# Value products of the decode stage: from a split fp32r form over all output partitions to plain fp32 in four strips of 32

## The reference, cut to what matters

```python
def sample_attn(q, k, v, lam, k_past, v_past, rel_bias):
    ...
    s_past = diff_logits(q, q_pos, k_past, jnp.arange(past, dtype=jnp.int32), rel_bias)
    s_new = diff_logits(q, q_pos, k, q_pos, rel_bias)
    w = diff_weights(jnp.concatenate([s_past, s_new], axis=-1), lam).astype(v.dtype)
    return (jnp.einsum('bhqk,bkhe->bqhe', w[..., :past], v_past)
            + jnp.einsum('bhqk,bkhe->bqhe', w[..., past:], v))
```

## Time and profile before

| what | value |
|---|---|
| timed runs | 2044.92, 2045.65, 2045.75 us; median 2045.65 |
| span of the profiled execution, first to last instruction | 2043.6 us |
| median less that span | 2.05 us |
| instructions | 36009 |
| mean granted TensorE clock | 0.997 |
| sampled stage, from the first key transposes to the last value product | about 835 to 1077 us of the span |

### The profile page before, as it was taken

The page is one execution under the profiler, slowest core; times in us unless marked ns, Lnnn a source line. Parts: engine busy times, 40 slices in busy tenths (PEclk is TensorE's granted clock), DMA queues, the critical chain, the costliest instruction groups (busy, mean ns, idle before and its releaser), DMA issues. The chain is left out here.

```text
span 2043.6 us, 36009 instructions
## 1 busy us (share of the span) xinstructions
PE 1993.2 (98%) x11888; PEld 1850.2 (91%) x11888; DVE 1375.8 (67%) x2932; ACT 998.2 (49%) x1770; POOL 131.7 (6%) x158
## 2 busy tenths in 40 slices
PE   6999999999999999799999999999999999999998
PEld 6999999999999999688878799999999998989896
DVE  6766776767676767678785376675757474847476
ACT  5756575757565757677874242222313141313133
POOL 0000000000000000145560000000000000000000
PEclk9999999999999999999999999999999999999999
DMA  6411111112121112788873131111112020202012
GB/s 199 144 57 54 57 53 56 53 60 59 50 59 50 59 52 87 261 306 304 316 268 92 38 93 42 53 42 42 52 32 62 22 72 22 72 21 69 6 53 99
DMA packets 167453, 183.26 MB, mean 90 GB/s; under 512 B 11045, under 2 KB 139589, under 8 KB 167349
## 3 DMA queue, kind: packets, MB, share of 16 engines
q1 hardware_dynamic: 166137, 181.24, 27.1%
q10 hardware_dynamic: 1212, 0.81, 0.1%
HBM read 162.82 MB, written 24.46 MB: 92 GB/s over the span
## 5 line engine op out<-in xcount | busy, mean ns | idle before, releaser
L1250 PE MATMUL ps<-h_hi,w_hi 128*128 128x384 f32 (+1 forms) x1152 | 386.7, 336 | 5.0 <-DVEq L967 3.4
L1250 PE MATMUL ps<-h_hi,w_lo 128*128 128x384 f32 (+1 forms) x1152 | 376.5, 327 | 0.0
L1250 PE MATMUL ps<-h_lo,w_hi 128*128 128x384 f32 (+1 forms) x1152 | 376.4, 327 | 0.0
L2456 PE MATMUL ps<-h_hi,f_w_hi 128*128 128x320 f32 (+1 forms) x1136 | 370.7, 326 | 0.8 <-PEq L1579 0.8
L2456 PE MATMUL ps<-h_hi,f_w_lo 128*128 128x320 f32 (+1 forms) x1136 | 370.4, 326 | 0.0
L2456 PE MATMUL ps<-h_lo,f_w_hi 128*128 128x320 f32 (+1 forms) x1136 | 370.2, 326 | 0.0
L2535 ACT ACTIVATE yc<-ps,f_prm 128x384 f32<-128x384 f32 x144 | 93.5, 653 | 560.6 <-PE ps L2456 400.0
L2436 PE MATMUL ps<-d_hi,act 128*128 128x512 f32 x816 | 257.0, 390 | 0.5 <-issue 0.5
L1250 PEld LDWEIGHTS ps<-h_hi,w_hi 128*128 128x128 f32 x1152 | 217.0, 188 | 9.0 <-issue 4.0
L1250 PEld LDWEIGHTS ps<-h_lo,w_hi 128*128 128x128 f32 x1152 | 217.1, 188 | 0.6
L1250 PEld LDWEIGHTS ps<-h_hi,w_lo 128*128 128x128 f32 x1152 | 216.8, 188 | 0.0
(11 more groups left out here) (310 smaller groups left out, 3525.2 us busy)
## 6 DMA issues: line engine op xcount, KB each, us to landing
k<-in_cache_k SPq DMA_DIRECT2D x64, 512.0 KB, 5.9
v_raw<-in_cache_v SPq DMA_DIRECT2D x64, 512.0 KB, 4.7
w_raw<-in_w_in SPq DMA_DIRECT2D x48, 512.0 KB, 4.0
f_raw<-in_w_up SPq DMA_DIRECT2D x48, 512.0 KB, 4.0
f_raw<-in_w_down SPq DMA_DIRECT2D x24, 512.0 KB, 3.5
bias<-bias_tiles_dram SPq DMA_DIRECT2D x8, 576.0 KB, 3.6
merged_dram<-mg SPq DMA_DIRECT2D x8, 544.0 KB, 2.7
ow_raw<-in_w_out SPq DMA_DIRECT2D x8, 512.0 KB, 7.5
```

The lines of the kernel that those rows point to most:

```text
L1250: last_ = pe.matmul(bank(s)[:, 0:n], w[:, W_SLOT[g], k, :], x[:, k, off:off + n], start=(k == 0 and i == 0), stop=(k == KT - 1 and i == 2))
L2456: l_ = pe.matmul(ps[:, e % 6, 0:n], w[:, p, k, :], x[:, k, off:off + n], start=(k == 0 and i == 0), stop=(k == KT - 1 and i == 2))
```

## The change

Values stay as they were loaded, in plain fp32. `v_hi`, `v_lo`, `vn` and the split of the weights are gone, with their ScalarE, VectorE and GpSimd instructions. `pt_sb` holds 64 weight columns a page. Each page has two matmuls, one for each half of the value columns: heads 0 to 3 need only rows 0 to 31 of the weights and value columns 0 to 511, heads 4 to 7 rows 32 to 63 and columns 512 to 1023, so the stationary operand is 32 columns and the output 32 partitions. Half `hf` of an even or an odd page goes into strip `2 * hf + n % 2` of one bank; four strips of 32 partitions. `o2` is one bank of 512 columns, `copy_o2` copies 512 columns, `fold_heads` makes 4 transposes, and `fold_rows` adds an even and an odd strip in two instructions.

```diff
-SPLIT_AT = {2: (0, 1), 3: (2,), 4: (3,), 5: (4, 5), 6: (6,), 7: (7,)}
-PV_EARLY = {5: (2,)}
-PV_AT = {4: (0, 1), 5: (), 6: (3,), 7: (4,), 8: (5, 6, NPAGES)}
+PV_EARLY = {}
+PV_AT = {4: (0, 1, 2, 3), 5: (), 6: (), 7: (), 8: (4, 5, 6, NPAGES)}
...
-    pt_both = sb("pt_both", [128, NPAGES + 1, 2, NS], F32R, 158784)
-    o2s = sb("o2s", [128, D], F32, 163392)
+    pt_sb = sb("pt_sb", [128, NPAGES + 1, NS], F32, 158784)
+    o2s = sb("o2s", [128, 512], F32, 163392)
...
+    def strip(hf, n):
+
+        q = 2 * hf + n % 2
+        return o2[32 * q:32 * q + 32, :]
...
-                for g in range(H):
+                for g in range(HH):
                     last = pe.transpose(o2[:, 128 * g:128 * (g + 1)], o2s[:, 128 * g:128 * (g + 1)], c.ident[:, :])
...
                 if n == NPAGES:
-                    pe.wait_ge(new_lo, 2)
-                elif n in POOL_PAGES:
-                    pe.wait_ge(vplo_done, pool_low(b, ("v", n)))
+                    pe.wait_ge(vn_in, 32)
                 else:
-                    pe.wait_ge(vlo_done, len(DVE_PAGES) * (b - 1) + DVE_PAGES.index(n) + 1)
+                    pe.wait_ge(v_in[n], 16 * b)
                 for hf in range(2):
                     cols = slice(512 * hf, 512 * (hf + 1))
-                    parts = (v_hi[:, n, cols], v_lo[:, n, cols]) if n < NPAGES else (vn[:, cols],)
-                    for x, v in enumerate(parts):
-                        last = pe.matmul(o2[:, cols], pt_both[:, n, :, :].rearrange("p a n -> p (a n)"), v,
-                                         start=(n == 0 and x == 0), stop=(n == NPAGES - 1 and x == 1))
+                    v = v_raw[:, n, cols] if n < NPAGES else vn_raw[:, cols]
+                    last = pe.matmul(strip(hf, n), pt_sb[:, n, 32 * hf:32 * hf + 32], v,
+                                     start=(n < 2), stop=(n in (NPAGES - 1, NPAGES)))
...
-                    if has(b, 1):
-                        for n in splits_of(b).get(h, ()):
-                            act.wait_ge(v_in[n], 16 * b)
-                            act.activation(v_hi[:, n, :], v_raw[:, n, :], ACT.Copy).then_inc(vhi_done, 1)
...
-                        for n in splits_of(b).get(h, ()):
-                            if n in POOL_PAGES:
-                                continue
-                            dve.wait_ge(vhi_done, 8 * (b - 1) + n + 1)
-                            dve.tensor_tensor(v_lo[:, n, :], v_raw[:, n, :], v_hi[:, n, :].bitcast(F32),
-                                              ALU.subtract).then_inc(vlo_done, 1)
```

More of the change, by code:

```diff
@@ L1406 @@
 OUT_LOW = [x for x in OUT_SPLITS if x[0] == "m" or x[1] >= 4]
-POOL_LAST = [x for h in range(H + 1)
-             for x in [("v", n) for n in SPLIT_AT.get(h, ()) if n in POOL_PAGES]
-             + [x for x in OUT_AT.get(h, ()) if x not in OUT_LOW]]
+POOL_LOW = [x for h in range(H + 1) for x in OUT_AT.get(h, ()) if x not in OUT_LOW]
 def sampled_and_out(nc, sb, sem, ins, outs, c):
@@ L1418, in sampled_and_out @@
     pt = ps[:, 5, :]
[L1419 to L1423, removed]
+    o2 = ps[:, 6, :]
+    ptn = ps[:, 7, 0:NS]
     v_raw = sb("v_raw", [128, NPAGES, D], F32, 32768)
@@ L1547, in bank_of, with pool_low @@
         return 3 if t == 0 else 0 if t % 2 else 2
[L1549 to L1559, removed]
+    def pool_low(what):
+        return POOL_LOW.index(what) + 1
     def all_turns(eng, body):
@@ L1809, in body @@
                         if h == 4:
-                            pe.wait_ge(ptlo_done, 2 * b)
+                            pe.wait_ge(pthi_done, 2 * b)
                         for n in PV_AT[h]:
@@ L1941, in body @@
                             queries(b + 1, 0)
-                    if h == HH + 1 and isinstance(b, int) and b == 1:
-                        act.wait_ge(vn_in, 32)
-                        act.activation(vn[:, :], vn_raw[:, :], ACT.Copy).then_inc(new_hi, 1)
                     if h == 1 and has(b, 2):
@@ L2056, in fold_rows @@
                 dve.wait_ge(ot_done, b + 1)
-                dve.reduce_sum(oT[:, :, bass.ds(DEC_T * b, DEC_T)], own_rows, mybir.AxisListType.X)                   .then_inc(ots_done, 1)
+                for hf in range(2):
+                    last = dve.reduce_sum(oT[:, HH * hf:HH * (hf + 1), bass.ds(DEC_T * b, DEC_T)], own_rows(hf),
+                                          mybir.AxisListType.X)
+                last.then_inc(ots_done, 1)
             def split_out(what, i):
@@ L2082, in body @@
                         keys(b, h)
-                    if h == 3 and has(b, 1):
-                        dve.wait_ge(pthi_done, 2 * b)
-                        dve.tensor_tensor(pt_lo[:, 0:NPAGES, :], pt.rearrange("p (n k) -> p n k", n=NPAGES),
-                                          pt_hi[:, 0:NPAGES, :].bitcast(F32), ALU.subtract).then_inc(ptlo_done, 1)
-                        dve.tensor_tensor(pt_lo[:, NPAGES, :], ptn, pt_hi[:, NPAGES, :].bitcast(F32),
-                                          ALU.subtract).then_inc(ptlo_done, 1)
                     if at_start(b) and h == 0:
@@ L2096, in body @@
                         queries(b, HH)
-                    if h == HH + 1 and isinstance(b, int) and b == 1:
-                        dve.wait_ge(new_hi, 2)
-                        dve.tensor_tensor(vn[NS:128, :], vn_raw[NS:128, :], vn[NS:128, :].bitcast(F32),
-                                          ALU.subtract).then_inc(new_lo, 1)
                     if h == HH and has(b, 0):
```

35 lines of the change are left out of this document (10 added, 25 removed).

## The result

Four runs of the changed kernel took 2016.15 to 2017.32 us, median 2016.62; four runs of the kernel before beside them had a median of 2045.29 us. The ratio of the times after to before is 0.9858, 95% interval 0.9844 to 0.9872: 28.7 us or 1.4% faster. The forecast was 2046.4 us. The time lies inside its range (2008 to 2076), and close to the 2012.5 us of the first rival.

A forecast was written before the change was run, and what follows sets the result against it. TensorE, busy 98% of the span, was taken as the bound. Seven bodies +4.2, last values 0.0 and body 7 -3.5 gave +0.7 us on the 2043.6 span; with 2.05 to the median, 2046.4 us, range 2008 to 2076.

The forecast's parts named there:

- the first rival: Value products: passes of four strips overlap fully, 4.3 us a sequence in place of 8.6; 2012.5 us, chance 0.29.
- The pairs of half-height matmuls: Earlier trace at 713.42: two matmuls on different array halves take 0.23 us together, as much as one full one.
- value products: Steady sequence: 18 fp32 matmuls on TensorE, only neighbouring passes overlapping, 8.6 us against 7.95, so +0.65 us.
- changes of shape, two runs: TensorE switching array shape, 0.09 us there and 0.14 back, for two value runs a body: +0.45 us.
- `fold_heads`: Transposes on TensorE fall from 8 to 4: -0.4 us a sequence.
- stalls: TensorE waits a sequence: +0.75 us at three heads newly without cover, -0.85 removed; sum taken as -0.1.
- The last values: Body 8: all 18 value matmuls as one run, with shape change and smaller fold, change the time by 0.0 us.
- Body 7: Its 2.41 us wait for `kt_lo` and half clock go, -4.1; output projection splits on uncovered heads, +0.6; together -3.5 us.
- the third rival: Passes overlap in pairs, but loads of narrow stationary operands no longer hide: +29 us on the forecast, 2075; chance 0.08.
- the second: Rival for the value products: strips served one after another, nothing overlaps, 15.5 us a sequence; 2102.7 us, chance 0.17.
- The readout of scores: Between scores: it needs 2.04 us, which a run of values with a head's transposes (3.9 + 0.8 or 1.7 + 0.8) covers.
- faster: Outcome for the whole kernel: a time lower by over 0.2%, given chance 0.38.

The follow-up runs named there:

- strip_by_strip: Changed kernel with the value matmuls of a run sorted by strip, so that passes of one strip stand behind one another; 2025.44 us, ratio 0.9897.
- pairs: Changed kernel with shorter runs of value matmuls: pages 0-1, 2-3 and 4-5 at h = 4, 5, 6, the rest at 8; 2022.83 us, ratio 0.9895.
- before_no_splits: Kernel before, with value splits made for the first sequence only (high parts alone) and reused later; TensorE's instructions unchanged; 2037.44 us, ratio 0.9959.
- gpsimd_only: Changed kernel with only the four GpSimd value subtractions a sequence kept, on a constant tile, read by nobody; 2027.42 us, ratio 0.9908.
- subtractions_kept: Changed kernel with four VectorE and four GpSimd value subtractions a sequence still made, read by nobody, no ScalarE copies; 2042.66 us, ratio 0.9984.
- two_in_a_row: Changed kernel with matmuls sorted by strip, but the new positions as their own run, so no strip has three in a row; 2018.42 us, ratio 0.9867.

## Why the prediction was wrong

**The step that failed.** "I take 8.6, because in all rows here matmuls start in the order of the program and a second fp32 pass starts when the first has streamed." The second half holds, the first doesn't carry over. The rows have no case where a pass waits for its strip while another strip is free. There TensorE doesn't hold back: the term is 4.3 us, its lower bound, and it was priced at twice that. The pairs of half-height matmuls had one pass each and couldn't tell. The Trainium skill, "TensorEngine Tiling (Array Packing)", Key Properties, says that tiles work independently; the trace agrees, four strips in one pass's 0.43 us. The Trainium skill, "TensorE: Matmul & The Clock Gate", Part 3, The mechanism, has matmuls start strictly in program order; here the measurement decides against it, since in strip_by_strip all four strips start at 947.8 (eight loads at 947.82), ahead of three waiting passes of the first.

**Term by term**, for a steady sequence:

| term | predicted | measured |
|---|---|---|
| value products | +0.65 | 4.3 - 7.95 = -3.65 |
| changes of shape, two runs | +0.45 | 0.09 in (942.21 to 943.33, against 1.03), 0.12 to 0.13 out: +0.43 |
| `fold_heads` | -0.4 | -0.4 |
| stalls | -0.1 (-1.5 to +0.8) | 24.7 - 21.7 - 2.2 = +0.8 |
| sum | +0.6 | -2.8 |

The 21.7 are 14.56 for the heads, 4.3, 0.43, 2.03 and 0.4. Pass price, the sum of the two changes of shape, and fold were right. (The 0.14 us back could not be read from the earlier trace rows: they give only four passes and the change together, 1.86 us.) The stalls came out at the top of their bounds. I counted three new heads without cover at 0.24 us, and 0.85 us of old stalls that go. There are four such heads in a row, 2.07, 2.15, 2.15 and 2.18 us from start to start, together 1.2 us over issue and shape; so only about 0.4 us of the old stalls went. The waits around the fold (0.42 and 0.44) stayed, as said.

**The rest.** The last values: predicted 0.0, measured 4.42 - 7.93 - 0.4 = -3.9, the same failed step. Body 7: the 2.41 us wait and the half clock went, as said. It gained 5.0 us, 2.2 more than a steady one, where 3.5 more were forecast (4.1 less 0.6). Loads from memory came in time: 338 GB/s at 0.91, and no wait for a page. Loads of the stationary operand, 0.11 us each, stayed hidden, since a round costs no more than a pass; so the third rival fell, and with 1.85 us for a run of 8 the second. The readout of scores stayed covered by the longer run, as said; pairs shows what it costs when it isn't. With 4.3 in place of 8.6 the sum is the first rival's 2012.5. From there to the measured 2016.6 go the stalls (7 x 0.9 = 6.3 us) and body 7 (1.3), less about 3.5 us that the first stretches, the last one and what lies outside gave beyond the sum.

**The relief.** I priced the work on the other engines at "the stalls they caused" and called that small. For the old stream this is right: before_no_splits gives 8 us. For the new stream it is wrong by its kind, not its size. The four corners:

| | splits made | no splits |
|---|---|---|
| old value products | 2045.3 | 2037.4 |
| strips | 2035.8 (old places), 2043.4 (new places) | 2016.6 |

The reading that fits all four: two limits stood nearly at one height, TensorE's issue (25.3 of 27.5 us), and the chain that makes `kt_lo`, with a VectorE that has 21.8 us of work and a GpSimd that holds it up. Either taken away alone leaves the other: 8 us, and 2 to 10. Both together give 28.7. With strips and the copies or subtractions put back, the second limit is in the subtractions, 26 us, more than in the copies, 7; and in both engines' subtractions together rather than one's (6.8 and 10.8). The parts were measured at the new places of the value products only. The chances of rival 1 (0.29) and of "faster" (0.38) were too low: the trace didn't decide between pairs and four at once, and I let one general impression of order decide.

**What stays open.** Whether the limit of two matmuls in a strip is one of matmuls or of passes: all matmuls here have two passes. Why the waits of 0.74 and 1.04 us for `C` go with a falling clock in gpsimd_only while those of 0.74 and 1.01 us in subtractions_kept don't (the matmuls behind them, at 948.04 for one, take their usual 2.00 us). And why, with the splits kept, the short runs beat the long ones by 8 us.

## What to carry to other kernels

A product with few output rows in plain fp32 paid here when it was spread over four strips of 32 output partitions, together with the relief of the helpers that it brings: count passes on the fullest strip, 0.43 us each for 512 columns, and keep at most two matmuls in a row on one strip; with two strips it only equalled the split form. Before pricing the relief of helper engines by the stalls they cause now, ask what they would bound once the main stream is shorter, and change both limits in one experiment and each alone. Try the long runs of independent matmuls where a chain on other engines must be waited out, and try them again elsewhere when that chain gets shorter.

## What the runs showed of the hardware

- Passes of plain fp32 matmuls overlap fully over four strips of output columns: 16 passes in 1.85 us, against 16 x 0.43 = 6.9 one after another.
- TensorE gets past a busy strip with up to four open passes (one running, three waiting), and with six it takes up the next strip only when two are done, 0.89 us late (strip_by_strip against two_in_a_row: 25.6 and 24.7 us a sequence).
- A GpSimd subtraction of 1.9 us holds up a VectorE operation with both inputs in SBUF that starts behind it: one of 0.16 us took up to 1.30 and ended with it, one of 1.21 took 2.92 and ended 1.08 after it. One with an input in PSUM kept its 1.23. Started first, the VectorE subtraction keeps its 1.22 us and the GpSimd one takes 2.93. The Trainium skill, "GPSIMD Engine Reference", Specifications, names just this: shared SBUF interfaces, with contention for VectorE instructions that have two SBUF inputs. The trace agrees for operations with two such inputs and for the one without.
